# RWKV low-rank stage: w1, a1 and g1 applied to the normed input and, scaled by the mix factors, to the shift difference, in place of mixed inputs

## The chip, the cores and the metric

One core of a Trainium2 chip runs the whole kernel. The metric is the device time of one execution in microseconds (us); shown is the median of three runs. The core's engines are TensorE (PE, with its weight loads as PEld), VectorE (DVE), ScalarE (ACT), GpSimd (POOL) and SyncE (SP, which only issues DMAs).

## The reference, cut to what matters

One step of a 4-layer recurrent trunk over T = 288 columns: 256 prompt tokens and 8 sample sequences of 4 tokens. Layers 0 and 3 use the RWKV-7 mixer (j = 0 and 1). Everything is float32.

```python
h = rmsnorm(x, norm_mix_pre)                       # x: the residual stream
prev = concatenate([shift0[:, None], h[:, :-1]], axis=1)
mixed = h[None] + (prev - h)[None] * rwkv_mix[j][:, None, None, :]
xr, xw, xk, xv, xa, xg = (mixed[s] for s in range(6))
r, k, v = einsum('sbtd,sde->sbte', stack([xr, xk, xv]), rwkv_w_rkv[j])
w_log = -softplus(-(w0 + tanh(xw @ w1) @ w2)) - 0.5   # w1: (1024, 64)
a = sigmoid(a0 + (xa @ a1) @ a2)                      # a1: (1024, 64)
g = sigmoid(xg @ g1) @ g2                             # g1: (1024, 128)
```

What follows (the delta-rule scan, the output projection) uses r, k, v, w_log, a and g and is not touched.

## The kernel before

Activations lie transposed: 1024 channels as KC = 8 tiles of 128 partitions by 288 columns, in twelve such buffers of one tensor `arena` (X, H, SQ and A0 to A8, the latter also called S[0] to S[8]). X is the residual stream, H the normed input, S[2] (Dx) the shift difference `prev - h`. All weights pass through `ring`, four slots of 128 x 2048, in the order of `weight_plan`; SP issues a slot's next DMA when its former content has been released. The big projections multiply in three float32r products, for which ACT rounds a slot to `w_hi` (`split_hi`) and DVE takes the rest to `w_lo` (`split_lo`). The low-rank weights w1, a1, w2, a2 and g1 are multiplied as plain float32, directly out of `ring`; such a matmul stands in the trace as two records.

Every engine has its own program in a fixed order; they meet at semaphores. The stage in question is the head of `rwkv(j)` on each engine.

- ACT: eight squares of X (`squares`), then `rms()`, which takes PE's sum of squares (`norm_stat`) and makes `rstd`; then `split_hi` of the first k slab. In layer 3 X only becomes ready tile by tile from DVE's `post_norm` of the FFN ahead, while ACT has `conv_state_out` of that FFN to do first.
- DVE: `pre_norm` makes H from X and `rstd` (8 instructions), four instructions make Dx, 16 `mix` instructions make the inputs of w1 and a1 (S[5], S[0]), `split_lo` of the first k slab, 8 more `mix` instructions for g1 (S[3]), and then `split_mix`, which makes the rounded input of the k projection.
- PE: 8 times a pair of matmuls for w1 and a1, each into 64 of one bank's partitions (L630, L631); 16 matmuls for w2 and a2 (L640), which wait for ACT's tanh; 8 for g1 (`linear_slab`, L488); one transpose (L564) and the k projection (L537 to L539).
- ACT then takes the results: tanh and copy of w1 and a1, 16 sigmoids for w2 and a2 (into S[6], S[1]), one for g1 (`hidden[2]`), and only then `split_hi(slabs[1])`, the second k slab.

The first tanh and the first sigmoid each stand behind an ACT_TABLE_LOAD, and the second load stands behind the wait for PE.

Of the kernel before, what the change touches and what calls it, by code (L numbers as in the profile page):

```python
# [49 lines left out]
def weight_plan():  # L50

    plan = []

    def ffn(i):
        for p in range(FPAIR):
            plan.append(("up", i, 0, p))
            plan.append(("up", i, 1, p))
        for m in range(4):
            for s in range(3):
                plan.append(("down", i, m, s))  # L60

    def rwkv(j):
        plan.append(("wa1", j))
        plan.append(("wa2", j))
        plan.append(("g1", j))
        plan.extend(("rkv", j, 1, m) for m in range(4))
        if j:
            plan.append(("v1",))
        plan.extend(("rkv", j, 2, m) for m in range(4))
        plan.extend(("rkv", j, 0, m) for m in range(4))  # L70
        plan.append(("g2", j))
        plan.extend(("rwo", j, m) for m in range(4))

# [19 lines left out]
def build(nc, A, OUT):  # L93
    ctx = ExitStack()
    with ctx:
# [243 lines left out]
        def slab_parts(key, slot):  # L339
# [3 lines left out]
            def v(o, k, n, rows=P):  # L343
                return slot[0:rows, o:o + k * n].rearrange("p (k n) -> p k n", k=k)
# [7 lines left out]
            if kind == "wa1":  # L352
                return [(v(0, 8, 64), cols(A["rwkv_w1"][key[1]], 0, 64)),
                        (v(512, 8, 64), cols(A["rwkv_a1"][key[1]], 0, 64))]
# [102 lines left out]
        def _(pe):  # L457
# [163 lines left out]
            def rwkv(j):  # L621
                norm_stat(0)
                sl1, sl2 = slab(), slab()
                w1 = sl1[:, 0:512].rearrange("p (k n) -> p k n", k=8)
                a1 = sl1[:, 512:1024].rearrange("p (k n) -> p k n", k=8)
                b = lin_bank()
                pe.wait_ge(*freed(b))
                for k in range(KC):
                    pe.wait_ge(sem("mix_ready"), after(pe, "mix_ready", 2))
                    nc.tensor.matmul(bk[b][0:64, 0:T], w1[:, k, :], S[5][:, k, :], start=(k == 0), stop=(k == KC - 1))  # L630
                    mm = nc.tensor.matmul(bk[b][64:128, 0:T], a1[:, k, :], S[0][:, k, :], start=(k == 0), stop=(k == KC - 1))  # L631
                mm.then_inc(filled["scalar"], 1)
                kw = result("scalar", b)
                free_after(filled["scalar"], kw + 1)
# [10 lines left out]
                wg1 = slab()[:, 0:1024].rearrange("p (k n) -> p k n", k=8)  # L645
                kg = linear_slab(lambda k, q: wg1[:, k, :], lambda k: S[3][:, k, :], 1, ("g1", j), "mix_ready")
                free_after(filled["scalar"], kg + 1)
# [1093 lines left out]
        def _(act):  # L1741
# [189 lines left out]

            def rwkv(j):
                slabs = [plan.index(("rkv", j, q, m)) for q in (1, 2, 0) for m in range(4)]
                if j:
                    squares(X, "x_ready")
# [576 lines left out]
        def _(dve):  # L2512
# [25 lines left out]
            def pre_norm(kind, i, name):  # L2538
                dve.wait_ge(sem("rstd_ready"), after(dve, "rstd_ready"))
                for c in range(KC):  # L2540
                    ins = stt(H[:, c, :], X[:, c, :], pcol(kind, i, c), rstd[:, :])
                    if name:
                        ins.then_inc(signal(name), 1)
                if not name:
                    name = "h_whole"
                    ins.then_inc(signal(name), 1)
                dve.wait_ge(sem(name), told[name])
# [99 lines left out]
            def rwkv(j):  # L2647
                slabs = [plan.index(("rkv", j, q, m)) for q in (1, 2, 0) for m in range(4)]
                pre_norm("mix_pre", 3 * j, None)
# [4 lines left out]
                tt(seqs(Dx)[:, :, :, 0], shiftT[:, j].rearrange("p b c -> p c b"), seqs(H)[:, :, :, 0], ALU.subtract).then_inc(signal("vector_chain"), 1)  # L2654
                dve.wait_ge(sem("vector_chain"), told["vector_chain"])
# [32 lines left out]
                dve.wait_ge(filled["scalar"], mark[("g1", j), 0] + 1)  # L2688
# [781 lines left out]
        def _(pool):  # L3470
# [159 lines left out]
            def rwkv(j):  # L3630
                pool.wait_ge(sem("h_whole"), after(pool, "h_whole"))
# [169 lines left out]
```

## Time and profile before

| what | before |
|---|---|
| median of 3 runs, us | 2252.76 (2252.04 to 2256.84) |
| profiled execution, us | 2256.73 |
| its span, us | 2254.5 |
| PE / PEld busy | 2037.8 (90%) / 1883.9 (84%) |
| DVE / ACT / POOL busy | 1483.7 (66%) / 978.6 (43%) / 549.3 (24%) |
| mean granted TensorE clock | 0.939 |

Times in the rows are counted from the start of the span. The first RWKV layer's low-rank stage lies at about 28 to 65 us, the second's at about 1647 to 1686 us. A busy share is a mean over stages with different limits, so the two stages are read from the instructions in order of time.

### The profile page before, as it was taken

How to read it: one execution, taken by the hardware profiler on the slowest of the kernel's cores; microseconds unless marked ns; L12 is line 12 of the kernel's file. 1: busy time of each engine (PE TensorE's matmuls, PEld its weight loads, DVE VectorE, ACT ScalarE, POOL GpSimd, SP SyncE). 2: the span in 40 equal slices, each digit the busy share in tenths (PEclk: the TensorE clock that was granted, in tenths of full speed). 3: DMA queues.
4: the chain of work that ended last, by engine and by line, in shares of the span. 5: the costliest groups of instructions: out<-in, count | busy, mean ns of one | idle time of the engine just before them, and what ended most of it. 6: DMA issues, size and time to landing. Idle time of an engine off the chain costs nothing.

```text
span 2254.5 us, 54677 instructions
## 1 busy us (share of the span) xinstructions
PE 2037.8 (90%) x23459; PEld 1883.9 (84%) x23459; DVE 1483.7 (66%) x2211; ACT 978.6 (43%) x1660; POOL 549.3 (24%) x934
## 2 busy tenths in 40 slices
PE   4999987999899787899989798899979899889998
PEld 2898867999878775899979777899958888679997
DVE  3785454896367557499645674799367765548963
ACT  3641134555356503455535433555345411345543
POOL 8000000453024111046201550256000200004630
PEclk9999998999989878899999887999989899989999
DMA  3430122455424323245534263354434201225552
GB/s 101 136 126 22 32 64 81 153 167 164 131 90 135 117 60 92 87 160 165 162 126 152 92 176 102 104 161 163 146 112 151 70 23 32 69 75 162 161 164 86
DMA packets 272111, 257.75 MB, mean 114 GB/s; under 512 B 30708, under 2 KB 267222, under 8 KB 271870
## 3 DMA queue, kind: packets, MB, share of 16 engines
q1 hardware_dynamic: 221472, 219.49, 30.3%
q10 hardware_dynamic: 45870, 20.44, 3.4%
q0 software_dynamic: 4528, 14.33, 2.3%
q8 instruction: 185, 3.03, 0.6%
q14 instruction: 56, 0.46, 0.1%
HBM read 235.69 MB, written 18.54 MB: 113 GB/s over the span
## 4 chain that ended last, share of the span: by engine, by line
PE 54%; DVE 6%; ACT 3%; issue 2%; ACTq 1%; POOL 0%; DVEq 0%; POOLq 0%
PE wide L537 7%; PE bank L537 7%; PE wide L539 7%; PE wide L538 7%; PE bank L539 6%; PE bank L538 6%; DVE arena L2528 3%; PE wide L548 2%; PE wide L745 1%; PE wide L730 1%; DVE arena L2525 1%; PE wide L742 1%; ACT arena L1752 1%; ACT w_hi L1752 1%; ACT rstd L1752 0%
## 5 line engine op out<-in xcount | busy, mean ns | idle before, releaser
L2528 DVE TENSOR_TENSOR w_lo<-ring,w_hi 128x2048 fp32r<-128x2048 f32 (+1 forms) x208 | 477.9, 2298 | 308.3 <-ACT w_hi L1752 294.0
L537 PE MATMUL wide<-arena_rounded,w_hi 128*128 128x288 f32 x1632 | 497.4, 305 | 35.6 <-DVE arena_rounded L2528 22.6
L537 PE MATMUL bank<-arena_rounded,w_hi 128*128 128x288 f32 x1632 | 490.0, 300 | 14.6 <-DVE arena_rounded L2528 11.4
L538 PE MATMUL wide<-arena_rounded,w_hi 128*128 128x288 f32 x1632 | 490.7, 301 | 0.0
L539 PE MATMUL wide<-arena_rounded,w_lo 128*128 128x288 f32 x1632 | 489.3, 300 | 0.0
L538 PE MATMUL bank<-arena_rounded,w_hi 128*128 128x288 f32 x1632 | 484.7, 297 | 0.0
L539 PE MATMUL bank<-arena_rounded,w_lo 128*128 128x288 f32 x1632 | 483.5, 296 | 0.0
L1752 ACT ACTIVATE w_hi<-ring 128x2048 fp32r<-128x2048 f32 (+1 forms) x208 | 391.7, 1884 | 141.1 <-PE wide L539 71.4
L537 PEld LDWEIGHTS wide<-arena_rounded,w_hi 128*128 128x128 f32 x1632 | 315.7, 193 | 46.5 <-issue 34.8
L537 PEld LDWEIGHTS bank<-arena_rounded,w_hi 128*128 128x128 f32 x1632 | 309.3, 190 | 18.2 <-DVE arena_rounded L2528 7.9
L2525 DVE SCALAR_TENSOR_TENSOR arena<-arena,pv 128x304 f32<-128x304 f32 (+2 forms) x512 | 302.7, 601 | 25.9 <-ACT arena L1752 10.4
L538 PEld LDWEIGHTS wide<-arena_rounded,w_hi 128*128 128x128 f32 x1632 | 316.2, 194 | 0.5
L539 PEld LDWEIGHTS wide<-arena_rounded,w_lo 128*128 128x128 f32 x1632 | 316.2, 194 | 0.0
L539 PEld LDWEIGHTS bank<-arena_rounded,w_lo 128*128 128x128 f32 x1632 | 310.4, 190 | 0.0
L538 PEld LDWEIGHTS bank<-arena_rounded,w_hi 128*128 128x128 f32 x1632 | 309.8, 190 | 0.6
L1752 ACT ACTIVATE arena<-wide 128x32 f32<-128x32 f32 (+4 forms) x347 | 109.7, 346 | 364.0 <-PE wide L539 163.4
L1752 ACT ACTIVATE arena<-bank 128x32 f32<-128x32 f32 (+4 forms) x292 | 84.6, 325 | 289.8 <-PE bank L539 175.9
L3601 POOL COPY arena<-arena 128x16 f32<-128x16 f32 (+1 forms) x200 | 160.7, 803 | 183.8 <-DVE arena L2525 170.2
L2528 DVE TENSOR_TENSOR arena<-arena 128x256 f32<-128x256 f32 (+6 forms) x326 | 176.2, 565 | 33.8 <-ACT arena L1752 28.8
L1752 ACT ACTIVATE arena<-arena 128x288 f32<-128x288 f32 (+4 forms) x329 | 171.2, 549 | 57.5 <-DVE arena L2525 35.8
L2525 DVE SCALAR_TENSOR_TENSOR arena<-arena,pv,rstd 128x288 f32<-128x288 f32 x128 | 63.5, 511 | 109.2 <-ACT rstd L1752 109.2
L3610 POOL COPY arena<-arena 128x2 f32<-128x2 f32 (+1 forms) x200 | 88.9, 445 | 165.9 <-ACT arena L1752 159.6
(498 smaller groups left out, 2708.0 us busy)
## 6 DMA issues: line engine op xcount, KB each, us to landing
ring<-in_ffn_w_up SPq DMA_DIRECT2D x88, 1024.0 KB, 5.1
ring<-in_ffn_w_down SPq DMA_DIRECT2D x32, 896.0 KB, 4.9
ring<-in_rwkv_w_rkv SPq DMA_DIRECT2D x24, 1024.0 KB, 5.1
ring<-in_ffn_w_down SPq DMA_DIRECT2D x16, 1024.0 KB, 5.1
ring<-in_gdn_w_in SPq DMA_DIRECT2D x16, 1024.0 KB, 5.8
ring<-in_hgrn_w_in SPq DMA_DIRECT2D x16, 1024.0 KB, 5.4
ring<-in_rwkv_w_o SPq DMA_DIRECT2D x8, 1024.0 KB, 5.2
sraw<-in_state_rwkv_wkv POOLq DMA_DIRECT2D x32, 128.0 KB, 3.1
```

The lines of the kernel that those rows point to most:

```text
L537: nc.tensor.matmul(out, wh, xh, start=first, stop=False)
L538: nc.tensor.matmul(out, wh, xl, start=False, stop=False)
L539: return nc.tensor.matmul(out, wl, xh, start=False, stop=last)
L548: mm = nc.tensor.matmul(bk[b][:, 0:T], ones[:, :], src[:, c, :], start=(c == 0), stop=(c == KC - 1))
L730: mm = nc.tensor.matmul(bk[b][rows, c * 64:c * 64 + 64], LT[g][rows, c, :], TF[g][rows, c, :], start=True, stop=True)
L742: nc.tensor.matmul(bk[b][rows, c * 32:c * 32 + 32].rearrange("p (b t) -> p b t", t=h), tt_[g][rows, c, :], halves(EL[g][rows, c, :], h, 0) ...
L745: mm = nc.tensor.matmul(bk[b][rows, 256 + c * 32:288 + c * 32].rearrange("p (b t) -> p b t", t=h), EL[g][rows, c, :], halves(tt_[g][rows, ...
L1752: return nc.scalar.activation(out, in_, f, bias=bias, scale=scale)
L2525: return V.scalar_tensor_tensor(out=out, in0=a, scalar=s, in1=b, op0=o0, op1=o1)
L2528: return V.tensor_tensor(out, a, b, op)
L3601: G.tensor_copy(s[:, :, 0:lead], hv[:, :, :, c]).then_inc(signal("hist_in"), 1)
L3610: G.tensor_copy(lv[:, 0, :, c], ext[:, NPR:NPR + lead])
```

## The change

w1 and a1 now lie side by side, eight blocks of 128 columns, in the first half of their ring slot; g1 lies likewise. ACT writes a second copy of these weights into the second half of each slot, every block scaled by its mix factors (`scale_weights`). PE multiplies the plain weights with H and adds the scaled weights times Dx in the same bank. The 24 `mix` instructions for w1, a1 and g1 are gone. g1 comes ahead of w2 and a2 in the plan, on PE and on ACT. `pre_norm` signals each H tile; Dx has its own semaphore.

```diff
     def rwkv(j):
         plan.append(("wa1", j))
+        plan.append(("g1", j))
         plan.append(("wa2", j))
-        plan.append(("g1", j))
...
             if kind == "wa1":
-                return [(v(0, 8, 64), cols(A["rwkv_w1"][key[1]], 0, 64)),
-                        (v(512, 8, 64), cols(A["rwkv_a1"][key[1]], 0, 64))]
+                return [(v(0, 8, 128)[:, :, 0:64], cols(A["rwkv_w1"][key[1]], 0, 64)),
+                        (v(0, 8, 128)[:, :, 64:128], cols(A["rwkv_a1"][key[1]], 0, 64))]
...
             def rwkv(j):
                 norm_stat(0)
...
+                wa1, wg1 = [sl[:, 0:2048].rearrange("p (e k n) -> p e k n", e=2, k=8) for sl in (slab(), slab())]
+                bs = [lin_bank(), lin_bank()]
+                for b in bs:
+                    pe.wait_ge(*freed(b))
                 for k in range(KC):
-                    pe.wait_ge(sem("mix_ready"), after(pe, "mix_ready", 2))
-                    nc.tensor.matmul(bk[b][0:64, 0:T], w1[:, k, :], S[5][:, k, :], start=(k == 0), stop=(k == KC - 1))
-                    mm = nc.tensor.matmul(bk[b][64:128, 0:T], a1[:, k, :], S[0][:, k, :], start=(k == 0), stop=(k == KC - 1))
...
+                    pe.wait_ge(sem("h_tile"), after(pe, "h_tile"))
+                    for b, w in zip(bs, (wa1, wg1)):
+                        nc.tensor.matmul(bk[b][:, 0:T], w[:, 0, k, :], H[:, k, :], start=(k == 0), stop=False)
+                for b, w in zip(bs, (wa1, wg1)):
+                    pe.wait_ge(sem("weights_scaled"), after(pe, "weights_scaled"))
+                    if w is wa1:
+                        pe.wait_ge(sem("shift_difference"), after(pe, "shift_difference"))
+                    for k in range(KC):
+                        mm = nc.tensor.matmul(bk[b][:, 0:T], w[:, 1, k, :], S[2][:, k, :], start=False, stop=(k == KC - 1))
+                    mm.then_inc(filled["scalar"], 1)
+                    kg = result("scalar", b)
+                    free_after(filled["scalar"], kg + 1)
+                kw = kg - 1
+                sl2 = slab()
                 pe.wait_ge(drained["scalar"], kw + 1)
...
-                wg1 = slab()[:, 0:1024].rearrange("p (k n) -> p k n", k=8)
-                kg = linear_slab(lambda k, q: wg1[:, k, :], lambda k: S[3][:, k, :], 1, ("g1", j), "mix_ready")
-                free_after(filled["scalar"], kg + 1)
...
+            def scale_weights(j):
+
+                for key, parts in (("wa1", ((3, 0, 64), (4, 64, 128))), ("g1", ((5, 0, 128),))):
+                    n = plan.index((key, j))
+                    act.wait_ge(landed[n % RING], landed_at[n])
+                    w = ring[:, n % RING, 0:2048].rearrange("p (e k n) -> p e k n", e=2, k=8)
+                    for k in range(KC):
+                        for i, a, b in parts:
+                            ins = fn(w[:, 1, k, a:b], w[:, 0, k, a:b], ACT.Copy, scale=pcol("mix", j * 6 + MIX_ORDER[i], k))
+                    ins.then_inc(signal("weights_scaled"), 1)
+
             def rwkv(j):
                 slabs = [plan.index(("rkv", j, q, m)) for q in (1, 2, 0) for m in range(4)]
+                scale_weights(j)
                 if j:
                     squares(X, "x_ready")
                 rms()
...
                 act.wait_ge(drained["scalar"], n_taken["n"])
+                evac(hidden[2][:, :], ACT.Sigmoid)
                 for c in range(KC):
                     evac(S[6][:, c, :], ACT.Sigmoid, pcol("w0", j, c))
                     evac(S[1][:, c, :], ACT.Sigmoid, pcol("a0", j, c))
-                evac(hidden[2][:, :], ACT.Sigmoid)
                 split_hi(slabs[1])
...
-                for c in range(KC):
-                    mix(S[5][:, c, :], 3, c).then_inc(signal("mix_ready"), 1)
-                    mix(S[0][:, c, :], 4, c).then_inc(signal("mix_ready"), 1)
                 split_lo(slabs[0])
-                for c in range(KC):
-                    mix(S[3][:, c, :], 5, c).then_inc(signal("mix_ready"), 1)
                 split_mix(1, "SQ", "A8", {KC + 1: 1})
```

The first place is PE in layer 0, from the first w1 matmul on; `bank` and `wide` are result banks, `ring` the weights, `tm` the tanh of w1 and the copy of a1. Before, the g1 matmuls stand last:

```order
L630 MATMUL bank<-arena,ring 64x288 [waits drained_by_scalar,mix_ready,weights_landed1,weights_landed0]
L631 MATMUL bank<-arena,ring 64x288
L630 MATMUL bank<-arena,ring 64x288 [waits mix_ready]
L631 MATMUL bank<-arena,ring 64x288
...
L640 MATMUL bank<-tm,ring 128x288 [waits drained_by_scalar]
L640 MATMUL wide<-tm,ring 128x288 [waits drained_by_scalar] x2
...
L488 MATMUL bank<-arena,ring 128x288 [waits mix_ready,drained_by_scalar,weights_landed2]
L488 MATMUL bank<-arena,ring 128x288 [waits mix_ready] x7
```

Of the change, the same place:

```order
L630 MATMUL bank0<-arena,ring 128x288 [waits drained_by_scalar,h_tile,weights_landed1,weights_landed0]
L630 MATMUL bank1<-arena,ring 128x288
L630 MATMUL bank0<-arena,ring 128x288 [waits h_tile]
...
L636 MATMUL bank0<-arena,ring 128x288 [waits shift_difference,weights_scaled]
L636 MATMUL bank0<-arena,ring 128x288 x7
L636 MATMUL bank1<-arena,ring 128x288 [waits weights_scaled]
L636 MATMUL bank1<-arena,ring 128x288 x7
L647 MATMUL wide0<-tm,ring 128x288 [waits drained_by_scalar,weights_landed2]
```

Eight pairs of half-width matmuls and eight full ones, 24 instructions, became 32 full-width ones, all ahead of w2 and a2 (L647).

The second place is ACT in layer 3, from the conv state's DMAs of the FFN ahead to the first sigmoid of w2. Before:

```order
L1848 DMA out_sample_ffn_conv<-tm 88x8x128
L1752 ACTIVATE arena<-arena 128x288 [waits x_ready] x8
L1752 ACTIVATE rstd<-wide,eps 128x288 [waits filled_for_scalar]
L1752 ACTIVATE rstd<-rstd 128x288 [waits drained_by_scalar]
L1752 ACTIVATE w_hi<-ring 128x2048 [waits slab_used,weights_landed2,rstd_ready]
```

Of the change:

```order
L1852 DMA out_sample_ffn_conv<-tm 88x8x128
L1756 ACTIVATE ring<-ring,pv 128x64 [waits weights_landed3]
L1756 ACTIVATE ring<-ring,pv 128x64 x15
L1756 ACTIVATE ring<-ring,pv 128x128 [waits weights_landed0]
L1756 ACTIVATE ring<-ring,pv 128x128 x7
L1756 ACTIVATE arena<-arena 128x288 [waits x_ready] x8
L1756 ACTIVATE rstd<-wide,eps 128x288 [waits filled_for_scalar]
```

The 24 scalings stand ahead of the squares of X here; in layer 0 they stand behind the squares and ahead of `rstd`.

The third place is ACT in layer 0, behind tanh and copy; `arena` rows with `pv` are the sigmoids of w2 and a2, `tm` that of g1. Before:

```order
L1752 ACT_TABLE_LOAD [waits filled_for_scalar]
L1752 ACTIVATE arena<-bank,pv 128x288 [waits drained_by_scalar]
L1752 ACTIVATE arena<-wide,pv 128x288 [waits filled_for_scalar,drained_by_scalar] x2
...
L1752 ACTIVATE tm<-bank 128x288 [waits filled_for_scalar,drained_by_scalar]
L1752 ACTIVATE w_hi<-ring 128x2048 [waits weights_landed0,drained_by_scalar]
```

Of the change:

```order
L1756 ACT_TABLE_LOAD [waits filled_for_scalar]
L1756 ACTIVATE tm<-bank 128x288 [waits drained_by_scalar]
L1756 ACTIVATE arena<-wide,pv 128x288 [waits filled_for_scalar,drained_by_scalar] x2
...
L1756 ACTIVATE w_hi<-ring 128x2048 [waits weights_landed0,drained_by_scalar]
```

The table load now waits for g1's result, and g1's sigmoid stands ahead of the sixteen others.

## Rows read from the trace of the kernel before

**Rows 1.** The page: the chain that ended last, by engine.
```profile
PE 54%; DVE 6%; ACT 3%; issue 2%; ACTq 1%; POOL 0%; DVEq 0%; POOLq 0%
```

**Rows 2.** Timeline, PE, layer 0: start, length, instruction, [idle before <-releaser].
```profile
29.39 5.77 PE L548 MATMUL wide<-arena,ones 128*128 128x288 f32 x16 [0.99 <-ACT arena L1752]
...
43.83 0.71 PE L630 MATMUL bank<-arena,ring 128*64 128x288 f32 x1 [8.66 <-DVE arena L2525]
...
61.00 4.15 PE L488 MATMUL bank<-arena,ring 128*128 128x288 f32 x16
...
65.01 0.38 PE L537 MATMUL wide<-arena_rounded,w_hi 128*128 128x288 f32 x1
```

**Rows 3.** Timeline, DVE, layer 0.
```profile
36.28 3.52 DVE L2525 SCALAR_TENSOR_TENSOR arena<-arena,pv,rstd 128x288 f32<-128x288 f32 x8 [9.33 <-ACT rstd L1752]
...
42.73 6.96 DVE L2525 SCALAR_TENSOR_TENSOR arena<-arena,pv 128x288 f32<-128x288 f32 x16
...
67.64 2.29 DVE L2528 TENSOR_TENSOR w_lo<-ring,w_hi 128x2048 fp32r<-128x2048 f32 x1 [3.90 <-ACT w_hi L1752]
```

**Rows 4.** Timeline, ACT, layer 0.
```profile
28.80 2.77 ACT L1752 ACTIVATE arena<-arena 128x288 f32<-128x288 f32 x8
35.20 0.50 ACT L1752 ACTIVATE rstd<-wide,eps 128x288 f32<-128x288 f32 x1 [3.62 <-PE wide L548]
...
52.60 1.28 ACT L1752 ACT_TABLE_LOAD   x1 [0.88 <-PE wide L640]
53.90 0.50 ACT L1752 ACTIVATE arena<-bank,pv 128x288 f32<-128x288 f32 x1
...
65.25 0.41 ACT L1752 ACTIVATE tm<-bank 128x288 f32<-128x288 f32 x1 [2.84 <-PE bank L488]
```

**Rows 5.** Busy time of all engines in a stretch: PE, PEld, DVE, ACT, POOL, clock, DMA.
```profile
65.00:85.00 20.00, 20.00 (x152) 20.00 (x151) 15.19 (x27) 10.12 (x13) 0.00 (x0) 1.00 0.52 169
```

**Rows 6.** ACT groups by form, whole span: xcount | busy, mean ns | idle before.
```profile
L1752 ACT ACTIVATE arena<-arena 128x288 f32<-128x288 f32 x144 | 59.7, 439 | 17.0 <-DVE arena L2528 14.7
...
L1752 ACT ACTIVATE arena<-arena,pv 128x288 f32<-128x288 f32 x16 | 7.0, 521 | 0.0
...
L1752 ACT ACTIVATE us_all<-us_all 128x64 f32<-128x64 f32 x1 | 0.2, 238 | 0.0
```

**Rows 7.** Timeline, ACT: eight instructions with a scale from memory, back to back.
```profile
93.19 3.50 ACT L1752 ACTIVATE arena<-arena,pv 128x288 f32<-128x288 f32 x8
```

**Rows 8.** PE in four stretches: length, PE busy, granted clock, DMA share, GB/s.
```profile
35.20:39.50 4.30, 0.00 (x0) 1.00 0.00 0
39.50:49.65 10.15, 5.83 (x26) 0.50 0.00 1
1650.67:1654.03 3.36, 3.36 (x8) 0.50 0.27 70
1660.95:1667.60 6.65, 3.14 (x14) 0.50 0.26 73
```

**Rows 9.** Timeline, SP, ahead of layer 3: the second DMAs into the ring.
```profile
1632.63 0.48 SPq L3765 DMA_DIRECT2D ring<-in_rwkv_w  x1
```

**Rows 10.** Timeline, ACT, layer 3.
```profile
1648.93 0.38 ACTq L1848 DMA_DIRECT2D out_sample_ffn_conv<-tm  x1
...
1655.79 0.50 ACT L1752 ACTIVATE rstd<-wide,eps 128x288 f32<-128x288 f32 x1 [0.96 <-PE wide L548]
...
1674.13 0.50 ACT L1752 ACTIVATE arena<-wide,pv 128x288 f32<-128x288 f32 x1
```

**Rows 11.** Timeline, DVE, layer 3: the last tile of X.
```profile
1653.90 0.46 DVE L2528 TENSOR_TENSOR arena<-arena 128x288 f32<-128x288 f32 x1
```

**Rows 12.** Timeline, PE, layer 3.
```profile
1647.43 0.53 PE L564 MATMUL wide<-ident,arena 128*88 128x128 f32 x3 [0.93 <-ACT tm L1752]
1649.94 5.81 PE L548 MATMUL wide<-arena,ones 128*128 128x288 f32 x16 [1.98 <-ACT arena L1752]
...
1681.62 4.15 PE L488 MATMUL wide<-arena,ring 128*128 128x288 f32 x16
...
1685.63 0.38 PE L537 MATMUL bank<-arena_rounded,w_hi 128*128 128x288 f32 x1
```

More of the change, by code:

```diff
@@ L622, in rwkv @@
                 norm_stat(0)
[L623 to L627, printed above, removed]
-                for k in range(KC):
-                    pe.wait_ge(sem("mix_ready"), after(pe, "mix_ready", 2))
-                    nc.tensor.matmul(bk[b][0:64, 0:T], w1[:, k, :], S[5][:, k, :], start=(k == 0), stop=(k == KC - 1))
-                    mm = nc.tensor.matmul(bk[b][64:128, 0:T], a1[:, k, :], S[0][:, k, :], start=(k == 0), stop=(k == KC - 1))
-                mm.then_inc(filled["scalar"], 1)
-                kw = result("scalar", b)
-                free_after(filled["scalar"], kw + 1)
+                wa1, wg1 = [sl[:, 0:2048].rearrange("p (e k n) -> p e k n", e=2, k=8) for sl in (slab(), slab())]
+                bs = [lin_bank(), lin_bank()]
+                for b in bs:
+                    pe.wait_ge(*freed(b))
+                for k in range(KC):
+                    pe.wait_ge(sem("h_tile"), after(pe, "h_tile"))
[12 more added lines that the diff above has]
+                sl2 = slab()
                 pe.wait_ge(drained["scalar"], kw + 1)
@@ L2541, in pre_norm @@
                     ins = stt(H[:, c, :], X[:, c, :], pcol(kind, i, c), rstd[:, :])
[L2542 to L2545, printed above, removed]
                     ins.then_inc(signal(name), 1)
@@ L2648, in rwkv @@
                 slabs = [plan.index(("rkv", j, q, m)) for q in (1, 2, 0) for m in range(4)]
-                pre_norm("mix_pre", 3 * j, None)
+                pre_norm("mix_pre", 3 * j, "h_tile")
                 Dx = S[2]
@@ L2653, in rwkv @@
                 tt(seqs(Dx)[:, :, :, 1:NT], seqs(H)[:, :, :, 0:NT - 1], seqs(H)[:, :, :, 1:NT], ALU.subtract)
-                tt(seqs(Dx)[:, :, :, 0], shiftT[:, j].rearrange("p b c -> p c b"), seqs(H)[:, :, :, 0], ALU.subtract).then_inc(signal("vector_chain"), 1)
-                dve.wait_ge(sem("vector_chain"), told["vector_chain"])
+                tt(seqs(Dx)[:, :, :, 0], shiftT[:, j].rearrange("p b c -> p c b"), seqs(H)[:, :, :, 0], ALU.subtract).then_inc(signal("shift_difference"), 1)
+                dve.wait_ge(sem("shift_difference"), told["shift_difference"])
                 def mix(dst, i, c):
@@ L2679, in split_mix @@
                             split_lo(slabs[at[step]])
-                for c in range(KC):
-                    mix(S[5][:, c, :], 3, c).then_inc(signal("mix_ready"), 1)
-                    mix(S[0][:, c, :], 4, c).then_inc(signal("mix_ready"), 1)
                 split_lo(slabs[0])
-                for c in range(KC):
-                    mix(S[3][:, c, :], 5, c).then_inc(signal("mix_ready"), 1)
                 split_mix(1, "SQ", "A8", {KC + 1: 1})
-                dve.wait_ge(filled["scalar"], mark[("g1", j), 0] + 1)
                 split_mix(0, "A5", "A0", {2: 2, 6: 3, KC + 1: 4}, [S[3][:, c, :] for c in range(KC)])
@@ L3630, in rwkv @@
             def rwkv(j):
-                pool.wait_ge(sem("h_whole"), after(pool, "h_whole"))
+                pool.wait_ge(sem("h_tile"), after(pool, "h_tile", KC))
                 G.tensor_copy(spo_flat[:, 0:8], H[:, :, NPR - 1])
```

## The prediction

> **What bounds the kernel now.** I read first the chain that ended last: TensorE (PE) holds 54% of it, VectorE 6%, ScalarE (ACT) 3% [rows 1]. So the two low-rank stages count by how long they keep PE from its dense work, and I read them next, engine by engine in order of time. In layer 0 the last sum-of-squares matmul ends at 29.39 + 5.77 = 35.16 us; then PE waits 8.66 us for DVE, and the k projection starts at 65.01 [rows 2]. From there PE is busy for 20.00 of the next 20.00 us [rows 5]. What moves the start of k moves, by this, everything behind it: that start is what I forecast.
>
> What leads to it: rstd begins at 35.20 [rows 4], H takes 3.52 us, Dx lies between 39.80 and 42.73, the 16 mixes for w1 and a1 take 6.96 [rows 3]. PE follows them from 43.83. ACT takes w2 and a2 from 53.90 on, g1's matmuls run from 61.00 to 65.15 and k follows. DVE isn't late there: its next wait is 3.90 us long, for ACT's rounding of the second k slab [rows 3], and that rounding stands behind g1's sigmoid at 65.25 [rows 4]. Layer 3 repeats the pattern, with k at 1685.63 [rows 12].
>
> **What is removed.** DVE loses 24 mixes of 6.96 / 16 = 0.435 us, 10.4 us a layer [rows 3]. Sixteen of them stood between Dx and PE's first matmul, the other eight only beside other work. What DVE gains behind them I count at nothing: it still waits for the second k slab, which ACT rounds after the sigmoids.
>
> **What is added on PE.** g1's eight matmuls of 128 x 128 x 288 leave 16 records in 4.15 us at the full clock, 0.26 us each [rows 2]. The new stage has 32 such matmuls, 64 records: 64 x 0.26 = 16.6 us, against 4.15 for g1 before and about as much for the eight pairs. They can begin with the first H tile and follow at 1.04 us for a tile that DVE makes in 0.44, so PE isn't short of H; Dx is done after another 2.9 us [rows 3], and the H half takes PE 8.3 us. Neither new wait of PE (Dx, scaled weights) is met late.
>
> **What is added on ACT.** 24 scalings a layer, 16 of 64 columns and 8 of 128. The trace has no scaling of that size, so I build it from three forms: without a scale from memory 128x288 takes 439 ns and 128x64 238, with one 128x288 takes 521, so the operand adds 82 [rows 6]. Slope (439 - 238) / 224 = 0.90 ns a column: 320 ns for 64 columns, 377 for 128. Back to back, eight take 3.50 us, or (3.50 - 0.52) / 7 = 0.426 us from start to start, 0.095 less than one lasts [rows 7]: 0.225 and 0.282. 16 x 0.225 + 8 x 0.282 = 5.9 us. Lower bound, without the operand's price: 16 x 0.14 + 8 x 0.19 = 3.8; upper, no overlap: 16 x 0.32 + 8 x 0.377 = 8.1. I take 5.9, since the overlap was read from the same kind of instruction. The weights are there in time: SP's second pair of ring DMAs, g1's place now, goes out at 1632.6, 16.7 us ahead of the scalings [rows 9, 10].
>
> **Layer 0.** The squares end at 31.57 [rows 4]; the scalings follow to 37.5. Up to 35.2 they lie in ACT's wait for PE, the other 2.3 us delay rstd. First H tile: 36.28 + 0.51 + 2.3 = 39.1. PE idles 4 us from 35.16. Its clock fell at 39.5, 4.3 us after its last matmul, and came back at 49.65, 5.8 us after work had resumed; in layer 3 it was low for 3.36 us amid the sum of squares, and it came back 3.14 us after the work that began in the fourth stretch [rows 8]. I charge one stretch of 3.36 us at half clock, 1.7 us of lost work. g1 ends at 39.1 + 16.6 + 1.7 = 57.4. Behind it: 0.1 to ACT, the table load, 52.60 to 53.90 before, 1.3, g1's sigmoid 0.44, and then the w2 and a2 stretch, which runs at ACT's pace and ended on PE 7.1 us after ACT's first sigmoid (53.90 to 61.00) [rows 2, 4]. Sum 8.94: k at 66.3 against 65.0, **+1.3 us**.
>
> The Trainium skill, page ScalarE: Activation LUTs, section What ACT_TABLE_LOAD costs, gives 1.28 us for the load and another 1.38 of drain. The row here shows 1.30 from the load's start to the first activation [rows 4], so the drain isn't seen. By the page's price each layer would cost 1.4 us more and the sum would be 9.0 instead of 6.2, at about 2261.8.
>
> **Layer 3.** Here the scalings come ahead of the squares: ACT is through with the DMAs at 1649.3 [rows 10], the scalings end at 1655.2, when X, done at 1654.36 [rows 11], has been waiting. The first square is done 0.45 later, so the sum of squares starts at 1655.7 instead of 1649.94. PE will have been idle since 1647.96 [rows 12], 7.7 us, about as long as the idle times that brought the low clock; after these two it was low for 5.8 and 3.1 us of work [rows 8]: the mean, 4.5, costs 2.3. 16 records at 0.26 and 2.3 make 6.4, the end is 1662.1 against 1655.75. First H tile 1657.4 + 6.4 = 1663.8, 16.6 us, and 0.8 (half of 1.7, as a second fall may or may not come): 1681.2. Then 0.1 + 1.3 + 0.44 and 1681.62 - 1674.13 = 7.5 [rows 10, 12]: k at 1690.5 against 1685.6, **+4.9 us**.
>
> Sum +6.2 us. The profiled execution, from which every duration comes, took 2256.73 us for a span of 2254.5, 4 us more than the median; it would become 2262.9. Set on the median 2252.76: **2259.0 us**. A measurement of this kernel tells about 0.2%, 4.5 us, from no change.
>
> **What may differ.** The scalings between 3.8 and 8.1 us: about -2.1 to +2.2 a layer. The clock in layer 0 between none and two low stretches: -1.7 to +1.7; in layer 3 -3.1 to +1.5. A low clock when k begins, not seen before, since g1's dense matmuls stood there: 0 to +1.7 a layer. All at one end: -2.8 or +17, so 2250 to 2270.
>
> **Rivals.**
> - *PE keeps its full clock.* The idle time before the first matmul shrinks from 8.7 to 4 us in layer 0, and what follows is dense. Then 1.7 falls away in layer 0 and 2.3 + 0.8 in layer 3: +1.4, 2254.2 us, not slower beyond 0.2%. For it: in the first stretch of rows 8 the clock held for 4.3 us without a matmul. Against it: it was already low in layer 3's sum of squares, after a shorter gap with three turns in it [rows 8, 12]. It decides where the clock stays at 2.4 GHz through the first H matmuls of both layers. The Trainium skill, page TensorE: Matmul & The Clock Gate, Part 1, speaks for the forecast in layer 3: the low clock is the default that only activity lifts. Chance 0.22.
> - *DVE's freed time arrives at k.* If k's start hung on DVE's splitting, it could come 10.4 us earlier in each layer: 2252.76 - 20.8 = 2232. Against it: k begins right behind g1's matmuls, and DVE ends its splitting and waits [rows 2, 3]. It would decide only if PE had nothing ahead of k. Chance 0.05.
> - *k begins at the half clock in both layers.* The dense g1 matmuls no longer stand behind the ACT-paced stretch, so k's first 3.36 us may run at 1.2 GHz: +1.7 twice, 2262.4 us. For it: g1 at the full clock came right behind that stretch before; against it: the records of k are dense too, and part of that stretch may again be past the low clock. Chance 0.18.
>
> **How the numbers follow.** The forecast has 0.50, the rivals 0.22, 0.05 and 0.18; 0.05 is for what I don't see. Three quarters of the forecast, the third rival and half of the rest lie over 2257.3: slower 0.375 + 0.18 + 0.025 = 0.58. A quarter of the forecast, most of the first rival and part of the rest lie within 0.2%: 0.33. Faster: the second rival, and what is left, 0.09. The range, 2250 to 2268, spans the first and third rival and most of the bounds; it leaves out the second and the sum of all upper ends.
>
> **What would show it.** Right: in layer 0 rstd about 2.3 us later, in layer 3 the sum of squares starting near 1655.7; 64 records for w1, a1 and g1 in 17 to 19 us; the second table load right behind g1; k 1 to 2 us later in layer 0 and 3 to 6 in layer 3; no new idle time on PE between the H and the Dx half. Wrong: scalings well under 0.2 us or over 0.3 each, k earlier than before in either layer, DVE no longer waiting for the second k slab, or a shift of k that is not found again at the end of the layer.

## The result: slower by 0.6%, more than twice what was forecast

Run side by side, the kernel after took 2266.35 us (median of 8, 2261.69 to 2277.98) and the kernel before 2254.58 (8 runs). The ratio is 1.0063, 95% interval 1.0042 to 1.0083: 14.2 us on 2250 (9.5 to 18.7; by the two medians 11.8), where 6.2 was forecast. The direction is as forecast and the time lies in the range; the size is off.

| what | before | after |
|---|---|---|
| profiled execution, its span, us | 2256.73, 2254.5 | 2261.69, 2260.0 |
| PE / PEld busy, us | 2037.8 / 1883.9 | 2049.7 / 1893.8 |
| DVE / ACT / POOL busy, us | 1483.7 / 978.6 / 549.3 | 1461.9 / 991.0 / 545.1 |
| mean granted TensorE clock | 0.939 | 0.944 |

The two profiled executions differ by 5.0 us and the medians by more; why one profile can't settle this is the point of the experiments. First the stage itself. The start of k is counted here and below from the transpose just ahead of it (L564).

PE in layer 0 (timeline: start, us, engine and line, operation, count, idle time ahead and what ended it). Line numbers have moved: ACT's helper is L1756 here, DVE's are L2541 and L2544. The last line is that of the kernel before.

```profile
29.95 4.12 PE L548 MATMUL wide<-arena,ones 128*128 128x288 f32 x16 [1.08 <-ACT arena L1756]
39.93 10.81 PE L630 MATMUL bank<-arena,ring 128*128 128x288 f32 x32 [5.87 <-DVE arena L2541]
50.58 7.92 PE L636 MATMUL bank<-arena,ring 128*128 128x288 f32 x32
...
67.42 0.30 PE L564 MATMUL wide<-ident,spo 128*72 128x128 f32 x1
67.48 0.38 PE L537 MATMUL wide<-arena_rounded,w_hi 128*128 128x288 f32 x1
```
```profile
64.98 0.27 PE L564 MATMUL wide<-ident,spo 128*72 128x128 f32 x1
```

The 64 records follow each other without a gap: Dx and the scaled weights are there in time. They end at 58.5, 18.6 us after they began (forecast 18.3), and k starts 8.9 us later (forecast 8.94), at 67.42 against 64.98 before. ACT's side of it:

```profile
29.36 2.78 ACT L1756 ACTIVATE arena<-arena 128x288 f32<-128x288 f32 x8
32.05 6.26 ACT L1756 ACTIVATE ring<-ring,pv 128x64 f32<-128x64 f32 x24
38.20 0.49 ACT L1756 ACTIVATE rstd<-wide,eps 128x288 f32<-128x288 f32 x1
...
58.58 1.28 ACT L1756 ACT_TABLE_LOAD   x1 [3.10 <-PE bank L636]
59.87 0.41 ACT L1756 ACTIVATE tm<-bank 128x288 f32<-128x288 f32 x1
...
68.86 1.92 ACT L1756 ACTIVATE w_hi<-ring 128x2048 fp32r<-128x2048 f32 x1
```

The 24 scalings take 6.26 us (forecast 5.9). They hold rstd back, since PE was through with the squares at 34.07. From the start of the second table load to the activation behind it 1.29 us pass, 1.30 before [rows 4]; the drain of which the Trainium skill speaks (ScalarE: Activation LUTs, What ACT_TABLE_LOAD costs) isn't seen here either.

Layer 3, ACT and then PE; the last three lines are those of the kernel before, ACT, PE and DVE:

```profile
1647.45 0.50 ACT L1756 ACTIVATE rstd<-wide,eps 128x288 f32<-128x288 f32 x1 [0.84 <-PE wide L548]
...
1650.92 6.27 ACT L1756 ACTIVATE ring<-ring,pv 128x64 f32<-128x64 f32 x24 [0.81 <-ACT tm L1756]
1657.09 2.77 ACT L1756 ACTIVATE arena<-arena 128x288 f32<-128x288 f32 x8
1664.72 0.50 ACT L1756 ACTIVATE rstd<-wide,eps 128x288 f32<-128x288 f32 x1 [4.87 <-PE wide L548]
```
```profile
1657.67 7.02 PE L548 MATMUL wide<-arena,ones 128*128 128x288 f32 x16 [8.14 <-ACT arena L1756]
1666.47 8.00 PE L630 MATMUL wide<-arena,ring 128*128 128x288 f32 x32 [1.78 <-DVE arena L2541]
1674.30 7.92 PE L636 MATMUL wide<-arena,ring 128*128 128x288 f32 x32
...
1691.15 0.30 PE L564 MATMUL wide<-ident,spo 128*72 128x128 f32 x1
```
```profile
1645.89 0.50 ACT L1752 ACTIVATE rstd<-wide,eps 128x288 f32<-128x288 f32 x1 [0.84 <-PE wide L548]
1685.61 0.27 PE L564 MATMUL wide<-ident,spo 128*72 128x128 f32 x1
1688.26 2.29 DVE L2528 TENSOR_TENSOR w_lo<-ring,w_hi 128x2048 fp32r<-128x2048 f32 x1 [3.92 <-ACT w_hi L1752]
```

The squares stand behind the scalings and PE waits 8.14 us for the first of them; before it waited 1.98 [rows 12]. Counted from the rstd of the FFN ahead, the first line of each kernel here, k comes after 43.70 us; in the kernel before it came after 39.72 (1645.89 to 1685.61): +4.0, forecast +4.9. DVE of the kernel after in the same two places:

```profile
70.81 2.29 DVE L2544 TENSOR_TENSOR w_lo<-ring,w_hi 128x2048 fp32r<-128x2048 f32 x1 [14.16 <-ACT w_hi L1756]
...
1694.55 2.29 DVE L2544 TENSOR_TENSOR w_lo<-ring,w_hi 128x2048 fp32r<-128x2048 f32 x1 [11.55 <-ACT w_hi L1756]
```

What DVE saved is turned into this wait. In layer 0 it is 14.16 us where it was 3.90 [rows 3]; in layer 3 it is 11.55 where it was 3.92, less because rstd, from which DVE starts, comes 7.4 us later there and k only 4.0.

So both stages did what was forecast, +2.4 and +4.0 us. About 8 us of the 14 by the ratio, or 5 of the 12 by the medians, are not in them.

### The profile page after: what moved, and what is told of

Read it like the earlier page. It is cut to its first block, busy times and chain, and to the rows that moved or that the text cites. A ratio compares the mean times of both kernels' runs of the same rounds, so it can differ in the third digit from the quotient of the medians.

```text
span 2260.0 us, 54741 instructions
## 1 busy us (share of the span) xinstructions
PE 2049.7 (91%) x23491; PEld 1893.8 (84%) x23491; DVE 1461.9 (65%) x2163; ACT 991.0 (44%) x1708; POOL 545.1 (24%) x934
## 4 chain that ended last, share of the span: by engine, by line
PE 54%; DVE 6%; ACT 3%; issue 2%; ACTq 1%; POOL 0%; DVEq 0%; POOLq 0%
PE wide L537 7%; PE bank L537 7%; PE wide L539 7%; PE wide L538 7%; PE bank L539 7%; PE bank L538 7%; DVE arena L2544 2%; PE wide L548 2%; PE wide L749 1%; PE wide L746 1%; PE wide L734 1%; DVE arena L2541 1%; ACT arena L1756 1%; ACT w_hi L1756 1%; DVE w_lo L2544 1%
## 5 line engine op out<-in xcount | busy, mean ns | idle before, releaser
L2544 DVE TENSOR_TENSOR w_lo<-ring,w_hi 128x2048 fp32r<-128x2048 f32 (+1 forms) x208 | 477.2, 2295 | 324.4 <-ACT w_hi L1756 309.9
L1756 ACT ACTIVATE w_hi<-ring 128x2048 fp32r<-128x2048 f32 (+1 forms) x208 | 391.9, 1885 | 141.4 <-PE wide L539 71.1
L2541 DVE SCALAR_TENSOR_TENSOR arena<-arena,pv 128x304 f32<-128x304 f32 (+3 forms) x464 | 282.1, 610 | 25.9 <-ACT arena L1756 10.5
L1756 ACT ACTIVATE arena<-wide 128x32 f32<-128x32 f32 (+4 forms) x347 | 109.7, 346 | 360.4 <-PE wide L539 164.5
L1756 ACT ACTIVATE arena<-bank 128x32 f32<-128x32 f32 (+4 forms) x292 | 84.6, 325 | 289.8 <-PE bank L539 175.7
L3607 POOL COPY arena<-arena 128x16 f32<-128x16 f32 (+1 forms) x200 | 154.8, 774 | 183.3 <-DVE arena L2541 169.7
L1756 ACT ACTIVATE arena<-arena 128x288 f32<-128x288 f32 (+4 forms) x329 | 171.1, 551 | 53.6 <-DVE arena L2541 35.0
L2544 DVE TENSOR_TENSOR arena<-arena 128x256 f32<-128x256 f32 (+6 forms) x326 | 175.1, 562 | 28.2 <-ACT arena L1756 23.1
L2541 DVE SCALAR_TENSOR_TENSOR arena<-arena,pv,rstd 128x288 f32<-128x288 f32 x128 | 63.5, 512 | 118.1 <-ACT rstd L1756 118.1
```

Source lines behind the costliest of these rows:

```text
L1756: return nc.scalar.activation(out, in_, f, bias=bias, scale=scale)
L2541: return V.scalar_tensor_tensor(out=out, in0=a, scalar=s, in1=b, op0=o0, op1=o1)
L2544: return V.tensor_tensor(out, a, b, op)
L3607: G.tensor_copy(s[:, :, 0:lead], hv[:, :, :, c]).then_inc(signal("hist_in"), 1)
```

## The experiments

**Where the time of the stage comes from.** e1 is the kernel after once more. e2 moves one line of ACT: the scalings stand behind the rounding of the first k slab, beside the H half on PE.

```diff
                 if j:
                     squares(X, "x_ready")
-                scale_weights(j)
                 rms()
                 split_hi(slabs[0])
+                scale_weights(j)
```

> The changed kernel once more, with another profile. Theory A (the start of k): in the first profile the k projection starts 2.5 us later in layer 0 (1.9 of it behind the squares) and about 4 us later in layer 3 counted from the rstd of the FFN ahead, some 5.5 us in all; the rest of the measured 12 us is scatter of stages that the change does not touch, so this run gives plus 4 to plus 9 us, and its profile again these two shifts. Theory B (a loss behind the stage): the denser TensorE work costs another 6 to 8 us later on, so plus 11 to plus 15 again, and the profile shows a place behind the stage that is slower in both profiles of the change than in the one of before.

> The changed kernel with the 24 scalings a layer behind the rounding of the first k slab instead of ahead of rstd. Theory A: rstd at 35.2 to 35.8 us in layer 0 and where it was before in layer 3, the scalings (6.2 us) end before TensorE is through with the H half (8 us), k about 3 us earlier than before in layer 0 and about 1.5 in layer 3: 3 to 6 us faster than before, 9 or more faster than the change. Theory B: the loss behind the stage stays, 2 to 4 us slower than before.

e1: 2265.94 us, ratio 1.0070 (1.0048 to 1.0093). e2: 2253.03, ratio 1.0011 (0.9990 to 1.0031). The scalings ahead of rstd cost 13 us by the medians; by the starts of k, 12. So k is late because the scalings stand ahead of rstd. ACT and PE of e2 in layer 0:

```profile
35.78 0.50 ACT L1756 ACTIVATE rstd<-wide,eps 128x288 f32<-128x288 f32 x1 [3.66 <-PE wide L548]
...
38.61 6.25 ACT L1756 ACTIVATE ring<-ring,pv 128x64 f32<-128x64 f32 x24
```
```profile
37.52 8.00 PE L630 MATMUL bank<-arena,ring 128*128 128x288 f32 x32 [1.78 <-DVE arena L2541]
45.36 7.92 PE L636 MATMUL bank<-arena,ring 128*128 128x288 f32 x32
...
62.20 0.30 PE L564 MATMUL wide<-ident,spo 128*72 128x128 f32 x1
```

ACT ends the scalings at 44.86, before PE wants them at 45.36, and PE waits 1.78 us in place of 5.87. k starts at 62.20, 2.8 us earlier than in the kernel before (64.98); in layer 3 it comes 36.2 us after the FFN's rstd instead of 39.7. And yet e2 isn't faster than the kernel before: 6 us gained in the stages don't arrive.

e3 puts the same scalings into the kernel before, at the place of the change, results unused. e4 is the kernel after without them and without PE's wait for them; it leaves the mix factors out.

```diff
 e3, PE, ahead of the first w1 matmul:
+                pe.wait_ge(sem("weights_scaled"), after(pe, "weights_scaled", 2))
 e4, PE, second half:
-   nc.tensor.matmul(bk[b][:, 0:T], w[:, 1, k, :], S[2][:, k, :], ...)
+   nc.tensor.matmul(bk[b][:, 0:T], w[:, 0, k, :], S[2][:, k, :], ...)
```

> The kernel before with nothing but the 24 scalings a layer added at the place the change has them (their results are not used; TensorE waits for them ahead of the first w1 matmul, which comes later anyway). Theory A: rstd 2.5 to 3 us later in layer 0 and 7 to 9 in layer 3, all of it carried on to k: plus 9 to plus 11 us, as much as or more than the change itself. Theory B: plus 9 to 11 too, but the change is then 3 to 5 us slower than this kernel.

> The changed kernel without the scalings: TensorE multiplies the plain weights with the shift difference, so the mix factors are left out of the low-rank stage. Theory A: as e2 within 1.5 us, 3 to 6 us faster than before; e3 and this one add up to the change. Theory B: 2 to 4 us slower than before, since TensorE does the same work as in the change.

e3: 2268.09, ratio 1.0067 (1.0041 to 1.0094). e4: 2254.42, ratio 1.0010 (0.9983 to 1.0036). The scalings alone make the kernel before as slow as the kernel after; without them the new stage is no faster than the old one, although its k comes 6.5 us earlier in the two layers together (counted as in the table below).

**Is the comparison biased, and which layer?** e5 is the kernel before once more, measured against itself. e6 is e2 with four of g1's scaled products ahead of w2 and a2 and four between their first pairs. e7 has the scalings late in layer 3 only. e8 is e2 again.

```diff
 e6, PE, in the loop over w2 and a2:
+                    if c < 4:
+                        mm = gate_part(4 + c)
 e7, ACT:
-                scale_weights(j)
                 if j:
                     squares(X, "x_ready")
+                else:
+                    scale_weights(j)
                 rms()
                 split_hi(slabs[0])
+                if j:
+                    scale_weights(j)
```

> The kernel before, unchanged, as a run of its own, for a second profile and as a measure of the comparison. So far the scalings cost 14 to 15 us by time (e1 against e2, e3 against before) and 10 to 12 by the start of k, and the change without them is 0 to 2 us slower than before though its k starts come 6 us earlier. Theory C (the first profile of before was one with a slow middle, and the measured 6 us are lost behind the stage by TensorE's clock in some executions): this run gives 0 plus or minus 3 us against before, and its profile shows the HGRN layer (rstd of the FFN of layer 1 to that of layer 2) at 245 to 246 us as in the other five, not 250.7. Theory D (the comparison favours the kernel before by some 6 us): plus 4 to plus 8 us.

> e2 with half of g1's matmuls on the shift difference put ahead of w2 and a2 and the other half between their first four pairs, where TensorE waits for ScalarE; g1's sigmoid comes after the eighth of the sixteen. The table load then waits for w2's first result, 4 us earlier. By the rows k starts 3 us earlier than in e2 in each layer (59 us in layer 0), so 6 us less than e2 if the time follows the starts of k one to one; 0 to 3 us less if what is won there is lost again behind the stage.

> The change with the scalings late in layer 3 alone. Theory A (time follows k): k as in e2 in layer 3 (36.2 us behind the FFN's rstd in place of 43.7), as in the change in layer 0; 7.5 us faster than the change, 4 to 5 slower than e2. If the scalings cost more than the start of k shows, then 9 to 11 faster than the change.

> e2 once more, so that it stands beside e5 to e7 on one chip and has a second profile. Theory C: 0 to 3 us slower than before once more, and its profile shows the 6 us won at k lost again in other places than in e2's (the scan of layer 3 took 325 us there from k to the FFN's rstd, 321 to 332 in the other five profiles). Theory D: the same time, and no such loss against the second profile of before.

e5: 2250.93, ratio 1.0006 (0.9990 to 1.0022), +1.4 us (-2.3 to +5.0): no bias is seen, and theory D's +4 to +8 is met at the interval's edge alone. e6: 2249.62, 1.0001 (0.9981 to 1.0020), though its k starts at 60.61 in layer 0 and 35.0 us after rstd in layer 3, 8.4 us earlier in all. e7: 2256.80, 1.0034 (1.0012 to 1.0055), between e1 and e2. e8: 2250.09, 1.0008 (0.9992 to 1.0024), as e2.

**Is it in the stretches behind the stage?** In the profiles so far three stretches of untouched work had lengths that differ from one execution to the next. For layer 0, from k's start to the end of the mixer (start:end, length, busy time and records of PE, PEld, DVE, ACT, POOL, granted clock, DMA share, GB/s), in e5 (the kernel before) and in the kernel after:

```profile
65.46:364.38 298.92, 279.25 (x5776) 252.37 (x5774) 183.07 (x287) 106.52 (x164) 9.11 (x13) 0.98 0.26 80
```
```profile
67.42:377.30 309.88, 289.36 (x5776) 258.01 (x5775) 183.27 (x287) 107.54 (x166) 9.12 (x13) 0.94 0.26 77
```

The same 5776 records; PE is idle for 19.7 and 20.5 us, and busy for 279 and 289 at a mean clock of 0.98 and 0.94. Ten of the 11 us are busy time of the same records, at a lower granted clock. Four single executions, two of the kernel before (e9, e10), one of after (e11) and one of e2 (e12), asked whether that goes with the kernel. They add up the three stretches: from k to the end of the mixer in layers 0 and 3, and the mixer of layer 1.

> The kernel before, one look. Open is where the part of the loss lies that the low-rank stages don't show: by the starts of k the change costs about 6 us (2 to 3 and 4), by time 12 to 16. The untouched stretches that scatter are layer 0 and layer 3 from k's start to the end of the mixer and the mixer of layer 1; their sum was 955.9 and 941.6 us in the two profiles of the kernel before, 947.1 to 969.2, mean 958.1, in the seven with the new PE stage. Theory C: part of the loss lies behind the stage, in these stretches; then the kernel before has them shorter, at 941 to 950. Theory S: they only scatter from execution to execution, and the sum lies anywhere in 940 to 970, around 955.

> The kernel before once more, a second look for the same question. Theory C: the three untouched stretches sum to 941 to 950 us. Theory S: anywhere in 940 to 970, around 955.

> The changed kernel, one look on the same chip. Theory C: the three untouched stretches sum to 957 to 961 us, as in its two profiles so far (957.7 and 960.1), 8 or more above those of the kernel before on this chip. Theory S: anywhere in 940 to 970. By both: rstd of layer 0 at 38.2, k of layer 0 at 66 to 68, k of layer 3 26.4 us behind its rstd.

> The changed kernel with the scalings behind the rounding of the first k slab, one look on the same chip. Theory C: k of layer 0 at 62 to 63, k of layer 3 26.4 us behind its rstd, and the untouched stretches sum to 954 to 962 us, which gives back what the stage gained. Theory S: anywhere in 940 to 970, no different from the kernel before.

The sums are 952.1 (e9), 948.0 (e10), 946.8 (e11) and 960.6 (e12). Theory C wanted 941 to 950 in e9 and 957 or more in e11; e10 and e12 lie where it has them, e9 and e11 don't, and e11 has the shortest sum of all kernels with the new stage in both layers. Its layer 0:

```profile
67.16:366.82 299.66, 280.18 (x5776) 252.56 (x5775) 183.08 (x287) 107.38 (x167) 9.13 (x13) 0.98 0.26 79
```

The kernel after can have this stretch as short as the kernel before. Over the nine profiles with the new stage in both layers up to here the mean sum is 957.1, over the four of the kernel before 949.4, with a scatter of 6 to 7: a hint of theory C's 8 us, and no proof. Of the 7.7 us between the means, 2.6 lie in layer 0, 3.0 in layer 3 and 2.1 in layer 1, whose mixer has two lengths. Here both kinds, each with a piece from the same place in the layer, e12 and then e6:

```profile
599.98:927.23 327.25, 278.65 (x3100) 241.70 (x3098) 198.90 (x316) 132.84 (x268) 66.72 (x96) 0.87 0.33 100
834.90:838.25 3.35, 3.35 (x68) 3.35 (x66) 0.75 (x2) 0.00 (x0) 0.00 (x0) 0.50 0.00 0
```
```profile
603.42:927.69 324.27, 277.44 (x3100) 240.77 (x3098) 199.04 (x316) 132.93 (x267) 66.83 (x96) 0.87 0.33 100
838.34:841.69 3.35, 3.35 (x112) 3.18 (x108) 2.31 (x5) 0.00 (x0) 0.00 (x0) 1.00 0.02 5
```

The mean clock of the layer is 0.87 in both, but in this piece e12 had the half clock and e6 the full one, and 5 us later e12 is some 2 us behind. So it also counts where the half clock falls. All four profiles of the kernel before have the short form and seven of the nine the long one. But so have four of the five in which the old stage is only delayed (e3, and e13, e14 and e17 below), and e18, so the long form doesn't need the new stage in both layers.

**A delay alone.** e13 to e17 lengthen the old stage (e16: that of e2) by small ACT instructions ahead of rstd, which nobody reads, n = 4 or 12.

```diff
-            def rms():
+            def rms(n=0):
                 act.wait_ge(filled["scalar"], take())
+                for _ in range(n):
+                    fn(pad[:, state["pad"], :], pv[:, 0, 0:64], ACT.Copy, scale=eps[:, 0:1])
+                    state["pad"] += 1
```

> The kernel before, with 4 additional small ACT instructions (64 columns, scale from memory, about 0.24 us each, results unused) ahead of rstd in layer 0: k starts about 1.0 us later in layer 0. Theory N (the loss outside the stages comes from the new PE stage, absent here): +1.0 us. Theory P (any shift of k's start against the rest costs some 5 us in PE's clock behind it): +5 to +7 us.

> The same with 12 such instructions in layer 0: k 2.9 us later there. Theory N: +2.9 us. Theory P: +6 to +9 us.

> The same with 12 such instructions in layer 0 and 12 in layer 3: k 2.9 us later in each, 5.8 in all, about what the change costs in its stages. Theory N: +5.8 us. Theory P: +10 to +14 us, as the changed kernel itself.

> The changed kernel with the scalings behind the rounding of the first k slab, and the same 12 instructions ahead of rstd in both layers: its stages end about where they end in the kernel before (k of layer 0 at 65 to 66 us, k of layer 3 29.4 us behind its rstd). Theory N: 5.8 us slower than without the delay, +6 to +9 us against the kernel before. Theory P: no slower than the kernel before by more than 4 us.

e13: 2253.06, 1.0008 (0.9993 to 1.0024). e14: 2252.73, 1.0010 (0.9996 to 1.0024). e15: 2261.63, 1.0042 (1.0022 to 1.0062). e16: 2261.09, 1.0049 (1.0032 to 1.0065; 6 runs). The twelve take what they were meant to, here in e16's layer 3:

```profile
1651.80 2.97 ACT L1757 ACTIVATE pad<-pv,eps 128x64 f32<-128x64 f32 x12 [0.84 <-PE wide L549]
1654.68 0.48 ACT L1757 ACTIVATE rstd<-wide,eps 128x288 f32<-128x288 f32 x1
```

Theory P fails for a delay in layer 0 alone: e13 and e14 cost about their own delay (1.8 and 2.3 us, at most 5.4 by either interval), where it had 5 to 7 and 6 to 9. It had e16 at 4 us or less; e16, whose k comes 4.2 us later than in the kernel before, both layers together, is 11 us slower. e15 agrees with neither: 9.5 us (5.0 to 14.0) for the 5.8 that its delays were meant to cost.

> The kernel before, with 12 additional small ACT instructions (results unused) ahead of rstd in layer 3 alone: k 2.9 us later there, layer 0 as before. Theory N (the loss outside the stages comes from the new PE stage, absent here): +2.9 us. Theory L (it comes with any change of layer 3's stage): +8 to +10 us.

> The new stage in layer 0 alone, with the scalings behind the rounding of the first k slab and half of g1's scaled products between the pairs of w2 and a2 (as in e6); layer 3 has the old stage, mixes included. k of layer 0 about 4.5 us earlier than before. Theory L: 4 to 5 us faster than the kernel before, which would make it the fastest of all. Theory N: no faster, within 3 us of the kernel before.

e18 has a branch on j in the plan, on PE, ACT and DVE: e6's stage for layer 0, the old one, mixes included, for layer 3. e17: 2255.53, 1.0015 (0.9990 to 1.0039), which is +3.4 (-2.3 to +8.8): theory N's 2.9 rather than theory L's 8 to 10. e18: 2248.28, 0.9990 (0.9969 to 1.0011): 2.3 us faster, between N's nothing and L's 4 to 5. It has the lowest ratio of the changed kernels, and isn't told apart from the kernel before.

**All of them side by side.** "Stages" is k's start in layer 0 plus the time from the FFN's rstd to k in layer 3, against the mean of four profiles of the kernel before (64.65 + 39.35 = 104.0 us); for after it is a mean of three. "Time" is (ratio - 1) x 2250 us. "Outside" is what is left.

| kernel | new stage in | stages | time | outside |
|---|---|---|---|---|
| after / e1 | both | +6.6 | +14.2 / +15.8 | 7.6 / 9.2 |
| e2 / e8 | both | -5.6 / -4.7 | +2.5 / +1.8 | 8.1 / 6.5 |
| e4 / e6 | both | -6.5 / -8.4 | +2.3 / +0.2 | 8.8 / 8.6 |
| e7 / e16 | both | 0.0 / +4.2 | +7.7 / +11.0 | 7.7 / 6.8 |
| e18 | layer 0 | -3.2 | -2.3 | 0.9 |
| e13 / e14 / e17 | none | +1.1 / +3.1 / +2.8 | +1.8 / +2.3 / +3.4 | 0.7 / -0.8 / 0.6 |
| e5 | none | +0.7 | +1.4 | 0.7 |
| e3 / e15 | none | +10.3 / +4.0 | +15.1 / +9.5 | 4.8 / 5.5 |

A single value is good to 4 or 5 us, but the eight with the new stage in both layers lie between 6.5 and 9.2, mean 7.9, and the other seven have a mean of 1.8. So a shift of k does go through to the end one for one, about: among the eight, the stages span 15 us and the time 15.6. On top of it, the new stage in both layers costs 6 us more (give or take 3) somewhere else. The same table can be split another way: the ten kernels in which both layers' stages were touched, by the new stage or by a delay (e3, e15), lie between 4.8 and 9.2 outside, the five with one layer touched or none between -0.8 and 0.9. That a change of both layers is enough, whatever it is, is a rival that no run here excludes.

## Why the prediction was right, and where it failed

- **Scalings, right.** 6.26 and 6.27 us for 24, against 5.9 built from three other forms.
- **Layer 0, right in mechanism, 0.6 to 1.1 us short.** rstd came 2.4 us later, seen from the end of the squares (forecast 2.3). k came 2.4 us later, 1.9 if counted from the squares, which began 0.56 later in this execution; forecast 1.3. The H half met the half clock for longer than the one stretch I charged:

```profile
39.93:45.40 5.47, 5.47 (x12) 3.85 (x13) 5.44 (x10) 2.46 (x2) 4.98 (x9) 0.50 0.00 0
45.40:50.60 5.20, 5.20 (x23) 4.10 (x22) 5.10 (x11) 0.00 (x0) 4.40 (x10) 0.98 0.01 3
...
62.70:66.10 3.40, 3.40 (x13) 3.01 (x13) 0.00 (x0) 3.21 (x7) 0.00 (x0) 0.50 0.06 21
66.10:67.50 1.40, 1.40 (x9) 0.73 (x7) 0.00 (x0) 1.30 (x4) 0.00 (x0) 1.00 0.00 0
67.50:87.50 20.00, 20.00 (x151) 20.00 (x152) 15.20 (x27) 11.00 (x15) 0.00 (x0) 1.00 0.49 160
```

(Windows of PE in the kernel after, columns as above.) PE had 5.47 us at 1.2 GHz, where 3.36 were charged: 1 us more of lost work, most of it made good by records of 15.8 / 64 = 0.247 us where I took 0.26. The second low stretch lies in w2 and a2, at ACT's pace, and costs nothing: from the last of the 64 records to k it is 8.92 us here and 8.93 in layer 3, where the clock stayed at 1.00.
- **Layer 3, right, 0.9 us too high.** The sum of squares ran at half clock first, as forecast, and a bit longer than forecast (7.02 us against 6.4). Then the clock came back and stayed, through both halves:

```profile
1657.67:1661.00 3.33, 3.33 (x7) 2.47 (x8) 0.00 (x0) 2.19 (x7) 0.00 (x0) 0.50 0.00 0
...
1666.47:1674.30 7.83, 7.83 (x32) 6.15 (x33) 7.76 (x12) 2.46 (x2) 4.53 (x5) 1.00 0.11 28
1674.30:1682.20 7.90, 7.90 (x35) 5.94 (x33) 7.83 (x24) 0.81 (x2) 0.90 (x2) 1.00 0.52 167
1682.20:1691.15 8.95, 8.28 (x33) 4.46 (x33) 0.80 (x3) 8.38 (x16) 0.00 (x0) 1.00 0.43 139
1691.20:1711.20 20.00, 20.00 (x152) 20.00 (x152) 15.19 (x27) 11.00 (x15) 0.00 (x0) 1.00 0.38 114
```

The 64 records took 15.8 us, not 17.4. That the low clock stands until activity lifts it (the Trainium skill, TensorE: Matmul & The Clock Gate, Part 1) agrees: 0.50 for the first 3.33 us of work after the wait of 8.14, 1.00 once the sum was done.
- **Rival 1** (PE keeps its full clock) fails in layer 0, where the H half began at 0.50, and in layer 3's sum of squares; it held in layer 3's two halves. **Rival 2** (DVE's time arrives at k) falls: 14.16 us of waiting. **Rival 3** (k at half clock) falls: 1.00 from 67.50 on, and from 1691.20 on in layer 3.
- **What failed** is the step from the stage to the time: "What moves the start of k moves, by this, everything behind it: that start is what I forecast." The forecast of that start was good (+6.2, measured +6.4 in this profile and +6.6 over three); the time moved by 14. Everything outside of the two stages stood in the sum at nothing; the runs put 7.6 us there in the kernel after, 6.5 to 9.2 in all eight with the new stage in both layers. I had PE busy for 20 of 20 us behind k [rows 5] and took that for a fixed duration. It isn't one: PE was busy for 279 us in one execution and for 289 in another with the same records, at a clock of 0.98 and 0.94. That the 7.6 us are of this kind is not shown. They come with the new stage whether its scalings are early, late or absent (e1, e2, e4) and wherever its k starts (e16); the kernel before pays little or nothing outside when its k is delayed in one layer (e13, e14, e17), and about 5 us, not clear of nothing, when it is delayed in both (e3, e15). That the time came out inside the range is luck: the range was made from bounds on the scalings and on the clock in the stages and at k's start, not for a loss elsewhere.
- **The base** was uncertain too: three runs agreed within 5 us, but the kernel before took 2239.55 to 2263.18 in 35 executions on one chip, and its profile was a long one (2254.5; the other three 2237.2 to 2243.0).

**What stays open.** Where the 6 to 8 us lie is not shown, nor what brings them. The sums of the stretches don't decide it: their mean is 957.1 with the new stage, but e11 has a short one, and the five profiles of old stages that were only delayed (e3, e13, e14, e15, e17) have a mean of 955.1, near that of the new stage. A fourth stretch scatters too, the mixer of layer 2: 241.8 to 251.5 us with the old stage, 245.1 to 245.7 with the new one; its mean, 245.7 in the kernel before and 245.4 in the nine, adds nothing.

Nor is the mean clock lower. Over all executions e2, e8 and e6 were granted 0.946 to 0.947, the kernel before beside them 0.941 and 0.942. Most of that rise is the stage itself: in layer 0 it ran at 0.77 in e5 and at 0.94 in e2, and both layers together save 24 to 27 us at half clock, which would raise the mean by 0.005 to 0.006. What is missing to that is about 0.002 at most in e2, e4, e6, e7 and e8: as an estimate, up to 10 us more at half clock elsewhere, and half of that, 5 us, in lost work. So the clock's total can hold a part of the loss; in layer 1 it mattered as well where the half clock fell.

e18, with 0.9 us outside, points to layer 3's new stage or to a change of both layers together, but by one comparison that is good to 5 us. Of the old stages that were delayed in both layers, e3's interval (9.2 to 21.2 us) holds its stages' 10.3, while e15's (5.0 to 14.0) begins 1 us above its stages' 4.0 and holds the 5.8 that was meant. A run with the new stage in layer 3 alone is missing.

## What to carry to other kernels

Work that is taken off one engine on the way to a start isn't gained when another must do something new ahead of the same start: place the new work behind the instruction that releases the next stage (one line here, worth 13 us). A profile shows where a stage's start moves, to tenths of a microsecond; whether the total follows is for repeated runs, since the same work behind it took up to 4% longer from one execution to the next. So add a term for the untouched rest, with the scatter of that kernel's own executions as its size, and take several profiles before a few microseconds are put down to a stage.

## What the runs showed of the hardware that I had not expected

The same instructions, with the same idle time on PE, took 4% longer in one execution than in another, at a lower granted clock. Layer 3 from k's start to the end of the mixer, in e7 and in e4:

```profile
1675.60:1994.26 318.66, 292.67 (x5808) 261.35 (x5807) 183.24 (x287) 114.53 (x177) 26.59 (x16) 0.96 0.25 75
```
```profile
1677.50:2009.65 332.15, 306.56 (x5808) 270.19 (x5807) 183.80 (x287) 114.52 (x177) 26.58 (x16) 0.92 0.24 72
```

PE is idle for 26.0 and 25.6 us and busy for 292.7 and 306.6, at 0.96 and 0.92. At the same mean clock the mixer of layer 1 still came out at 324 or 327 us, and in the long form the half clock had fallen into work that was at the full clock in the short one. And a small activation whose scale comes from memory costs 0.26 us back to back (6.26 / 24, 64 and 128 columns mixed), where a single one of 128x64 without it lasts 0.238 [rows 6].
